# Stick-breaking attention: both heads of a pair go through each query tile together

## What is computed

```python
def stick_breaking_attention(q, k, v):
    """A[t,s] = beta[t,s] * prod_{s<j<t} (1 - beta[t,j]), s < t."""
    for t0 in range(0, seq, Q_BLOCK):            # Q_BLOCK = 128
        t1 = t0 + Q_BLOCK
        z = einsum('bhqd,bhkd->bhqk', q[:, :, t0:t1], k[:, :, :t1]) * scale
        log_stay = where(causal, log_sigmoid(-z), 0.0)
        log_between = cumsum(log_stay, reverse=True) - log_stay
        weights = where(causal, exp(log_sigmoid(z) + log_between), 0.0)
        outs.append(einsum('bhqk,bhkd->bhqd', weights, v[:, :, :t1]))
```

## Time and profile before

| | us |
|---|---|
| median of 3 runs | 2110.62 (2109.64 to 2113.6) |
| the profiled execution, whole | 2112.93 |
| its span | 2111.1 |
| TensorE matmul busy | 2040.8 (97%) |
| VectorE, ScalarE, GpSimd busy | 832.3, 749.7, 740.3 |
| mean granted TensorE clock | 0.983 |

### The profile page before, as it was taken

How to read it: one execution, slowest core, us unless ns; L and a number is a source line. 1 busy time by engine, 2 the same in 40 slices (tenths; PEclk the granted TensorE clock), 3 DMA queues, 4 the chain that set the end, 5 groups by cost and what they waited for, 6 DMA issues and landing times. The chain is left out here.

```text
span 2111.1 us, 25060 instructions
## 1 busy us (share of the span) xinstructions
PE 2040.8 (97%) x9903; PEld 1638.7 (78%) x9903; DVE 832.3 (39%) x1532; ACT 749.7 (36%) x1177; POOL 740.3 (35%) x311
## 2 busy tenths in 40 slices
PE   7999999999998999999899999999999899999998
PEld 6878777788877766667788888878888777888887
DVE  3427875622222355562322222245655413222221
ACT  4444444433333454553323222232222224222331
POOL 2315222355653221203244444423222133444442
PEclk9999999999999999999999999999999999999999
DMA  4214122133332211102233323322222123323331
GB/s 142 63 50 111 51 61 61 46 90 95 91 111 78 60 51 41 50 20 70 70 91 99 100 90 100 90 78 62 61 60 61 31 71 89 100 90 100 90 100 50
DMA packets 267558, 159.62 MB, mean 76 GB/s; under 512 B 6089, under 2 KB 265393, under 8 KB 267442
## 3 DMA queue, kind: packets, MB, share of 16 engines
q1 hardware_dynamic: 267442, 158.02, 25.7%
HBM read 155.91 MB, written 2.10 MB: 75 GB/s over the span
## 5 line engine op out<-in xcount | busy, mean ns | idle before, releaser
L227 POOL TENSOR_TENSOR weight_lo<-weight_stage,weight_hi 128x1024 fp32r<-128x1024 f32 x303 | 739.4, 2445 | 1328.9 <-ACT weight_hi L217 1200.4
L217 ACT ACTIVATE weight_hi<-weight_stage 128x1024 fp32r<-128x1024 f32 x303 | 319.1, 1055 | 394.1 <-PE bank L244 365.4
L244 PE MATMUL bank<-a_hi,weight_lo 128*128 128x512 f32 x512 | 201.6, 394 | 6.6 <-DVE a_lo L346 6.6
L244 PE MATMUL bank<-hidden_hi,weight_lo 128*128 128x512 f32 x512 | 201.9, 394 | 0.0
L244 PE MATMUL bank<-hidden_hi,weight_hi 128*128 128x512 f32 x512 | 201.8, 394 | 0.0
L244 PE MATMUL bank<-hidden_lo,weight_hi 128*128 128x512 f32 x512 | 201.8, 394 | 0.0
L244 PE MATMUL bank<-a_lo,weight_hi 128*128 128x512 f32 x512 | 200.7, 392 | 0.0
L244 PE MATMUL bank<-a_hi,weight_hi 128*128 128x512 f32 x512 | 200.5, 392 | 0.0
L694 PE MATMUL bank<-a_hi,weight_lo 128*128 128x512 f32 (+1 forms) x464 | 197.0, 425 | 3.1 <-DVE a_lo L346 3.1
L1927 DVE TENSOR_TENSOR x_t<-x_t,bank 128x512 f32<-128x512 f32 x128 | 82.3, 684 | 268.0 <-PE bank L244 268.0
L695 PE MATMUL bank<-a_lo,weight_hi 128*128 128x512 f32 (+1 forms) x464 | 182.2, 393 | 0.0
(11 more groups left out here) (310 smaller groups left out, 3593.5 us busy)
## 6 DMA issues: line engine op xcount, KB each, us to landing
weight_stage<-in_mlp_w SPq DMA_DIRECT2D x128, 512.0 KB, 3.9
weight_stage<-in_w_in SPq DMA_DIRECT2D x57, 512.0 KB, 3.8
weight_stage<-in_hg_w_in SPq DMA_DIRECT2D x32, 512.0 KB, 4.0
weight_stage<-in_sb_w_qkv SPq DMA_DIRECT2D x24, 512.0 KB, 3.7
weight_stage<-in_w_mkv SPq DMA_DIRECT2D x8, 512.0 KB, 3.6
weight_stage<-in_w_out SPq DMA_DIRECT2D x8, 512.0 KB, 3.5
weight_stage<-in_sb_w_o SPq DMA_DIRECT2D x8, 512.0 KB, 3.5
weight_stage<-in_hg_w_o SPq DMA_DIRECT2D x8, 512.0 KB, 3.5
```

The source lines that it names most:

```text
L217: act.activation(self.hi[slot][:, :], self.stage[slot][:, :], ACT.Copy).then_inc(self.hi_done, 1)
L227: pool.tensor_tensor(self.lo[slot][:, :], self.stage[slot][:, :], self.hi[slot][:, :].bitcast(F32), ALU.subtract).then_inc(self.split_done, 1)
L244: last = pe.matmul(out, l, r, start=n == 0, stop=n == 3 * len(pairs) - 1)
```

## The change

Items are now ordered pair by pair: query tile i of the even head, then of the odd head. The loops run over m, a pair of items (32 of them), and:

- `score(m)` makes both heads' scores, in pieces of at most 256 columns, even head and odd head in turn, each to its own bank; it waits until all four sigmoids of m-1 are done.
- `weigh(m)` of TensorE follows each m: (i+1) x 2 matmuls of 128 columns, the even head's into partitions 0 to 63 of the out bank, the odd head's into 64 to 127, in turn.
- TensorE's loop: `fill(3)`, two turns, `score(m+1)`, `fill(3)`, pair work, `weigh(m-1)`.
- VectorE's loop: weigh(2m), both masks of the next m, weigh(2m+1). `lower` moves ahead of the weighing of tile 1.
- ScalarE's loop: four sigmoids, two keeps, then the pair's work; `put(p-1)` now stands in the loop's turn for tile 0.
- `sb_stay` has four buffers in place of two, `sb_beta` four in place of three, and the transposed weights go to eight tiles of `scratch`, one for each item.

```diff
-        stay = [sb(f"sb_stay{i}", [P, T]) for i in range(2)]
-        beta = [sb(f"sb_beta{i}", [P, T]) for i in range(3)]
+        stay = [sb(f"sb_stay{i}", [P, T]) for i in range(4)]
...
-        pt = [S.scratch[:, 0:4, :], S.scratch[:, 4:8, :]]
+        pt = [S.scratch[:, n, :] for n in range(8)]
...
-        items = [(h, i) for h in range(SB_HEADS) for i in range(NT)]
+        items = [(2 * p + r, i) for p in range(PAIRS) for i in range(NT) for r in range(2)]
         N = len(items)
+        M = N // 2
...
+                def score(m):
+                    p, i = divmod(m, NT)
+                    if i == 0:
                         pe.wait_ge(k_done, p + 1)
-                    wait(pe, sig, 2 * (n - 1))
-                    pe.matmul(score_banks[n % 2][:, 0:(i + 1) * P], qt[p % 3][r, i * P:(i + 1) * P],
-                              kt[p % 3][r, 0:(i + 1) * P], start=True, stop=True).then_inc(scored, 1)
+                    wait(pe, sig, 4 * m)
+                    for a in range(0, (i + 1) * P, 2 * P):
+                        b = min(a + 2 * P, (i + 1) * P)
+                        for r in range(2):
+                            rows = slice(r * 64, r * 64 + 64)
+                            last = pe.matmul(score_banks[r][:, a:b], qt[p % 3][rows, i * P:(i + 1) * P],
+                                             kt[p % 3][rows, a:b], start=True, stop=True)
+                            if b == (i + 1) * P:
+                                last.then_inc(scored, 1)
...
-                                            beta[n % 3][:, a + b * P:a + (b + 1) * P], S.eye)
+                                            beta[n % 4][:, a + b * P:a + (b + 1) * P], S.eye)
...
+                def weigh(m):
+                    p, i = divmod(m, NT)
+                    if i == 0:
                         wait(pe, out_lo, p)
                         pe.wait_ge(v_kept, p + 1)
-                    pe.wait_ge(kept, NT * (h + 1))
-                    r = h % 2 * 64
-                    for b in range(NT):
-                        last = pe.matmul(out_bank[r:r + 64, b * P:T], v_tok[p % 2][:, b, r:r + 64],
-                                         pt[h % 2][:, b, b * P:T], start=b == 0, stop=b == NT - 1)
-                    last.then_inc(weighed, 1)
+                    pe.wait_ge(kept, 2 * m + 2)
+                    for b in range(i + 1):
+                        for r in range(2):
+                            rows = slice(r * 64, r * 64 + 64)
+                            last = pe.matmul(out_bank[rows, i * P:(i + 1) * P], v_tok[p % 2][:, b, rows],
+                                             pt[(2 * m + r) % 8][:, b * P:(b + 1) * P], start=b == 0, stop=b == i)
+                            if b == i:
+                                last.then_inc(weighed, 1)
...
                 score(0)
-                score(1)
-                for n in range(N):
-                    p, j = divmod(n, 8)
+                for m in range(M):
+                    p, i = divmod(m, NT)
                     more = p + 1 < PAIRS
-                    if j == 4 and more:
+                    if i == 2 and more:
                         spread_k(p + 1)
                     fill(3)
-                    if n >= 1:
-                        turn(n - 1)
-                    if n + 2 < N:
-                        score(n + 2)
-                    if j == 1 and more:
+                    if m >= 1:
+                        turn(2 * m - 2)
+                        turn(2 * m - 1)
+                    if m + 1 < M:
+                        score(m + 1)
+                    fill(3)
+                    if i == 0 and more:
                         sums(p + 1, 0)
                         sums(p + 1, 1)
-                    if j == 7 and more:
+                    if i == 3 and more:
                         turn_v(p + 1)
-                    if n >= 6 and (n - 6) % NT == 0:
-                        weigh((n - 6) // NT)
+                    if m >= 1:
+                        weigh(m - 1)
+                turn(N - 2)
                 turn(N - 1)
-                weigh(SB_HEADS - 1)
+                weigh(M - 1)
...
-                    p, j = divmod(n, 8)
+                mask(1)
+                for m in range(M):
+                    p, i = divmod(m, NT)
                     more = p + 1 < PAIRS
-                    if n + 1 < N:
-                        mask(n + 1)
-                    weigh(n)
-                    if j == 2 and more:
+                    if i == 1 and p >= 1:
+                        lower(p - 1)
+                    weigh(2 * m)
+                    if m + 1 < M:
+                        mask(2 * m + 2)
+                        mask(2 * m + 3)
+                    weigh(2 * m + 1)
+                    if i == 0 and more:
                         root(p + 1)
-                    if j == 4 and more:
+                    if i == 2 and more:
                         scale_k(p + 1)
-                    if j == 5 and p >= 1:
-                        lower(p - 1)
...
+                    wait(act, weighed, 8 * (p - 1))
...
-                    wait(act, weighed, h - 1)
-                    act.activation(pt[h % 2][:, 0:i + 1, i * P:(i + 1) * P],
-                                   turn_banks[n % 2][:, 0:(i + 1) * P].rearrange("p (b t) -> p b t", b=i + 1),
+                    wait(act, weighed, n // 2 * 2 - 6)
+                    act.activation(pt[n % 8][:, 0:(i + 1) * P], turn_banks[n % 2][:, 0:(i + 1) * P],
                                    ACT.Copy).then_inc(kept, 1)
...
+                    act.wait_ge(weighed, 8 * (p + 1))
...
+                def sigmoids(n):
...
-                    if j == 0:
+                    wait(act, turned, n - 3)
+                    wait(act, scanned, n - 3)
...
+                    act.activation(stay[n % 4][:, a:T], src, ACT.Sigmoid, scale=minus[p][:, c:c + 1]).then_inc(sig, 1)
+                    act.activation(beta[n % 4][:, a:T], src, ACT.Sigmoid, scale=plus[p][:, c:c + 1]).then_inc(sig, 1)
+                for m in range(M):
+                    p, i = divmod(m, NT)
+                    more = p + 1 < PAIRS
+                    sigmoids(2 * m)
+                    sigmoids(2 * m + 1)
+                    if m >= 1:
+                        keep(2 * m - 2)
+                        keep(2 * m - 1)
+                    if i == 0 and p >= 1:
                         keep_v(p)
-                    if j == 0 and more:
+                    if i == 0 and more:
                         evict_q(p + 1)
-                    if j == 3 and p >= 1:
+                    if i == 0 and p >= 1:
                         put(p - 1)
-                    if j == 3 and more:
+                    if i == 1 and more:
                         evict_v(p + 1)
-                    if j == 6 and p + 2 < PAIRS:
+                    if i == 3 and p + 2 < PAIRS:
                         evict_k(p + 2)
```

More of the change, by code:

```diff
@@ L1516, in stick_breaking @@
         sq = [sb(f"sb_square{i}", [P, T]) for i in range(2)]
-        stay = [sb(f"sb_stay{i}", [P, T]) for i in range(2)]
-        beta = [sb(f"sb_beta{i}", [P, T]) for i in range(3)]
+        stay = [sb(f"sb_stay{i}", [P, T]) for i in range(4)]
+        beta = [sb(f"sb_beta{i}", [P, T]) for i in range(4)]
         left = [sb(f"sb_left{i}", [P, T + 1]) for i in range(2)]
@@ L1615, in turn @@
                         last = pe.transpose(turn_banks[n % 2][:, b * P:(b + 1) * P],
-                                            beta[n % 3][:, a + b * P:a + (b + 1) * P], S.eye)
+                                            beta[n % 4][:, a + b * P:a + (b + 1) * P], S.eye)
                     last.then_inc(turned, 1)
-                def weigh(h):
-                    p = h // 2
-                    if h % 2 == 0:
+                def weigh(m):
+                    p, i = divmod(m, NT)
+                    if i == 0:
                         wait(pe, out_lo, p)
                         pe.wait_ge(v_kept, p + 1)
-                    pe.wait_ge(kept, NT * (h + 1))
-                    r = h % 2 * 64
-                    for b in range(NT):
-                        last = pe.matmul(out_bank[r:r + 64, b * P:T], v_tok[p % 2][:, b, r:r + 64],
-                                         pt[h % 2][:, b, b * P:T], start=b == 0, stop=b == NT - 1)
-                    last.then_inc(weighed, 1)
+                    pe.wait_ge(kept, 2 * m + 2)
[6 more added lines that the diff above has]
+                                last.then_inc(weighed, 1)
                 norm.pe_spread(pe)
@@ L1698, in weigh @@
                     rev = slice(None, None, -1)
-                    dve.tensor_tensor_scan(left[n % 2][:, a:T][:, rev], stay[n % 2][:, a:T][:, rev], zeros[:, a:T],
+                    dve.tensor_tensor_scan(left[n % 2][:, a:T][:, rev], stay[n % 4][:, a:T][:, rev], zeros[:, a:T],
                                            1.0, ALU.mult, ALU.add).then_inc(scanned, 1)
@@ L1702, in weigh @@
                     dve.wait_ge(sig, 2 * n + 2)
```

(25 more changed lines are left out.)

1 line of the change is left out of this document (removed).

## The result

The changed kernel takes 2081.2 us (median of 4 runs, 2080.22 to 2086.01) beside 2112.11 for the kernel before (4 runs): ratio 0.986, 95% interval 0.984 to 0.988. 30.9 us are gone; 2087 was forecast, in a range of 2079 to 2101. The profiled execution (span 2084.2) was the slowest of the four, so it shows only 26.9 of them.

The account below looks back on a forecast made before the run. TensorE's list bounds the stage while filler lasts, VectorE's chain behind it. 186.7+3.4+1+33.3 = 224.4 us, less half the 3.4, plus 1.5 for the clock: 224 for 247.2, so 2087 us, range 2079 to 2101.

Parts of the forecast that it names:

- The bound: Whole stage: until item 50 it is as long as TensorE's own list of work; behind it VectorE's chain counts.
- the two waits that I feared: Loop: `put`, or a scan stretched beside GpSimd, holds sigmoids or masks; 1 to 1.5 us a pair, 2095, chance 0.08.
- Weighted sum, changed: TensorE's weighted sums: alternating column halves halve each record to 0.053 us; 3.3 us a pair for 4.6, saving 1.3.
- Score, changed: TensorE's scores: row halves overlap, 24 records at 0.107, four groups for eight; 3.8 us a pair for 6.7, saving 2.9.
- the last rival: Scores: weight loads of opposite row halves overlap too, 0.43 us a pair, 2084; no own chance, inside the forecast's 0.72.
- Filler part: Loop until the last filler: TensorE's entries sum to 186.7 us for 210.4, plus 3.4 for clock drops.
- the wait: Filler loop, tile 0: `put(p-1)` holds back tile 1's sigmoids; 0 to 0.3 us a pair, 1 us in all.
- the sign: Filler part: 187 to 192 us between 716 us and the last filler, TensorE busy throughout.
- the two drops of the clock: Filler part before the change: two granted-clock drops, 1.7 us lost each, 3.4 in all; whether they recur was left open.
- Behind the filler: End part, last filler to next stage: TensorE's gain buys nothing, VectorE's chain is late next; 33.3 us against 32.2.
- 1.5 more for a clock that may fall: End part, half idle: 1.5 us added to the stage's sum for a lower granted clock.
- Sum: Whole stage: 247.2 us becomes 224.4, then 224 after clock adjustments; 23 to 24 saved, median 2087.

Follow-up runs that it names:

- split scores: Changed kernel with the two heads' scores apart (turn, even head's score, turn, odd head's score), eight score groups a pair for four: 2114.1 us, ratio 1.000.
- the extra matmuls: Changed kernel plus four unread 512-column matmuls ahead of the turns of each m from 26 on: 2081.5 us; last filler matmul to next stage (E) 31.7 us.

## Why the prediction was right

**The bound.** TensorE's list sets the stage while filler lasts: right. Of the two waits that I feared there, none came; `put` holds up TensorE first at 901 us, for 0.37. The 1 us set aside for them was not needed.

**Weighted sum, changed.** 1.03 us for tile 3 (1.02 forecast), and a block order that loses half of it shows that it is the alternation. The Trainium skill's rule that a load overlaps a running matmul only where their row groups differ (TensorE: Matmul & The Clock Gate, Part 3, "The mechanism") does not hold for column halves in these runs: 16 loads and 16 matmuls in 1.03 us.

**Score, changed.** Mechanism right, size off. Row halves overlap, which no row of before had shown. The term was mis-sized: 24 records at 0.107, since I let the weight loads be the limit. The transposes from which I took that price have 128 moving columns too, and a record of 128 columns takes 0.107 by itself, so they showed nothing of loads. It measured 0.22+0.43+0.65+0.86 = 2.16 a pair for 2.57. That is 0.4 over 6.3 pairs, 2.6 us of gain that I had left out, and had named as the last rival. The Trainium skill's row on small-K matmuls (TensorE: Matmul & The Clock Gate, "Why this matters for your kernels"), by which slices on distinct row groups run concurrently, was the better guide. For two halves in fp32 this trace agrees: 0.85 us for both heads of tile 2, where one took 0.84. The remainder of the score's gain, fewer entries and exits, held: split scores cost 3.4 us more a pair (F longer by 21.3 us, over 6.3 pairs), 2.1 of it overlap, 1.2 four more groups.

**Filler part.** 191 us were forecast with drops and the wait, 183.4 came from the first score on, below the 187 to 192 that I had named as the sign. 2.6 of the gap are the loads, 3.4 the two drops of the clock, which I left in here and of which the sum took half off, 1 the wait. The drops did not recur: none of the thirteen kernels in the new order, split scores included, had one between 716 us and its last filler, while the clock of the kernel before is 0.98 there. So side by side scores are not what ended them. Why they are gone the runs don't tell; the sums have other neighbours now, and which of them matters was not tried. These 3.4 us of the gain are measured, but no step of the forecast's mechanism explains them.

**Behind the filler.** 33.3 forecast, 32.7 measured, against 32.8 before. That TensorE's gain buys nothing there is right, and VectorE is late next, as the waits on L1713 show. The 33.3 were walked at full clock, with 1.5 more for a clock that may fall. It did fall, and with the extra matmuls, at full clock, E is 31.7. So the walk was 1.6 us or more too long, and the low clock costs about 1 us here, 8 where the list is longer.

**Sum.** In the profiled executions the stage from first score to next stage shrank from 247.7 to 216.1, 31.6 us, where 23 to 24 were forecast. Of the 8 us that the forecast missed, 2.6 are the loads, 1.7 the half of the drops, 1 the wait and 2.1 the end part with its 1.5 for the clock; the rest, under 1 us, is not accounted for. The median shows the same: 5.8 us below the 2087 forecast. The whole span shrank by 26.9 only. 1.7 of the difference lie ahead of the stage, whose first score starts at 717.2 us in place of 715.5. Most of the rest is time in which stages without any edit ran at a lower clock in this execution:

```profile
1340.00:1420.00 80.00, 75.29 (x378) 63.64 (x378) 35.95 (x68) 22.86 (x33) 24.48 (x10) 0.91 0.24 68
1640.00:1780.00 140.00, 126.49 (x572) 103.71 (x572) 36.49 (x65) 42.13 (x58) 47.67 (x20) 0.91 0.25 72
```

The kernel before has 0.94 and 0.93 in these stretches. Two decimals are too few for the price. In stretches of 20 and 35 us, length times what the clock lacks of 1.00 adds up to 6.8 and 12.2 us for the changed kernel, and to 5.2 and 10.5 for the one before: some 3.3 us more are lost.

## What to carry to other kernels

In these kernels two matmuls that use half of the array each cost as one if they follow one another on opposite halves, in fp32 and for row and for column halves alike. So pair the heads, and alternate where a half has more than two matmuls. Count what TensorE enters and leaves as well: about 0.3 us for each group of half-array matmuls. Work that only fills gaps may be worth more where nothing else keeps TensorE busy: spread into the end part it took 1.7 us off the profiled stage, and nothing that the medians show by itself.

## What the hardware showed that I had not expected

- Weight loads of opposite row halves overlap: 16 loads of 128 columns in 0.97 us, 0.06 each, where whole-array matmuls of two columns, paced by such loads, follow at 0.11.
- Overlap doesn't need strict alternation. Two matmuls a half in blocks lose nothing (1.07 for 1.06 us), four lose 0.58 of 0.86 us (rows) or 0.48 of 0.85 (columns).
- Extra work can shorten a kernel: with six groups of four matmuls that nobody reads the clock of an end part was 1.00 throughout in place of 0.50 for 31 us, and the kernel went from 2114.1 to 2106.2 us.
